# Half a conditioning batch moves from TensorE to VectorE, and VectorE may take two parts of such work at one unit of weights

## The reference, cut to what matters

```
cond = silu(c)
for l in range(2):
    mod = cond @ w_ada[l] + b_ada[l]
    sh1, sc1, g1, sh2, sc2, g2 = split(mod, 6)
    h = rms_norm(x) * (1 + sc1) + sh1
    z = h @ w_in[l]                        # all heads' inputs
    out_a = diff_attention(...)            # 6 heads, two softmaxes each
    out_b = latent_attention(...)          # 6 heads, one softmax each
    out_c = spatial_gating(...)
    x = x + g1 * (concat(out_a, out_b, out_c) @ w_out[l])
    h = rms_norm(x) * (1 + sc2) + sh2
    x = x + g2 * conv_ffn(h, w_up, conv, w_down)
```

## Time and profile before

| | before |
|---|---|
| median of 3 runs | 2416.82 us |
| profiled execution, its own time | 2413.93 us |
| its span (first to last instruction) | 2412.1 us |
| TensorE busy | 2318.8 us (96%) |
| VectorE busy | 1876.2 us (78%) |
| ScalarE busy | 1142.0 us (47%) |
| GpSimd busy | 293.0 us (12%) |
| granted clock of TensorE, mean | 0.987 of full speed |

### The profile page before, as it was taken

One profiled execution on the slowest core, in us unless ns is written; L12 is line 12 of the kernel. 1 busy time (PEld: TensorE's weight loads), 2 busy tenths in 40 slices (PEclk: granted clock), 3 DMA queues, 4 the chain that ended last, 5 costly groups with the idle time before them and its releaser, 6 DMA issues.

```text
span 2412.1 us, 37004 instructions
## 1 busy us (share of the span) xinstructions
PE 2318.8 (96%) x14736; PEld 2017.7 (84%) x14736; DVE 1876.2 (78%) x2585; ACT 1142.0 (47%) x1605; POOL 293.0 (12%) x437
## 2 busy tenths in 40 slices
PE   5889999999999999999999999999999999999999
PEld 2568888988888888888887899998888888888888
DVE  1557877879999999999997696667998667766775
ACT  1333665454543454435544366545554345544553
POOL 4231321221101100110021020001110000000000
PEclk9899999999999999999999999999999999999999
DMA  9998787968989988999896766445896566656664
GB/s 334 318 299 280 252 283 251 316 202 279 290 289 346 317 279 280 314 361 285 276 305 195 249 213 188 137 147 161 280 295 213 191 190 189 189 192 191 188 190 148
DMA packets 442459, 596.94 MB, mean 247 GB/s; under 512 B 24188, under 2 KB 381744, under 8 KB 442032
## 3 DMA queue, kind: packets, MB, share of 16 engines
q1 hardware_dynamic: 386592, 392.54, 50.4%
q0 software_dynamic: 55296, 201.35, 25.9%
q10 hardware_dynamic: 400, 0.71, 0.1%
HBM read 592.42 MB, written 2.10 MB: 246 GB/s over the span
## 4 chain that ended last, share of the span: by engine, by line
PE 76%; DVE 12%; issue 4%; DMA 4%; ACT 3%; POOL 0%; DVEq 0%; ACTq 0%; POOLq 0%
PE bank L1158 76%; DVE wlo L1735 4%; DMA ada<-in_w_ada_dram 3%; DVE acc L1729 3%; ACT whi L1488 2%; DVE T L1754 1%; DMA raw<-in_w_in_dram 1%; DVE T L1818 1%; ACT hx L1556 0%; DVE yg L1761 0%; DVE r L1803 0%; DVE hx L1839 0%; DVE yv L1761 0%; ACT sc_s L1609 0%; DVE mx L1771 0%
## 5 line engine op out<-in xcount | busy, mean ns | idle before, releaser
L1158 PE MATMUL bank<-hx,whi 128*128 128x512 f32 (+1 forms) x4480 | 1360.6, 363 | 4.5 <-DVE hx L1964 3.0
L1735 DVE TENSOR_TENSOR wlo<-raw,whi 128x1024 fp32r<-128x1024 f32 (+2 forms) x774 | 908.3, 1180 | 397.0 <-ACT whi L1488 395.1
L1488 ACT ACTIVATE whi<-raw 128x1024 fp32r<-128x1024 f32 (+2 forms) x774 | 778.7, 1017 | 749.5 <-PE bank L1158 623.0
L1158 PE MATMUL bank<-hx,wlo 128*128 128x256 f32 x3840 | 1089.0, 284 | 28.7 <-DVE hx L1839 20.6
L1158 PEld LDWEIGHTS bank<-hx,whi 128*128 128x128 f32 x4480 | 803.3, 189 | 142.7 <-issue 5.8
L1158 PEld LDWEIGHTS bank<-hx,wlo 128*128 128x128 f32 x3840 | 731.4, 190 | 48.0 <-issue 21.3
L1158 PE MATMUL bank<-mx,whi 128*128 128x512 f32 (+1 forms) x2096 | 613.0, 356 | 1.2 <-DVE xT L1785 1.2
L1158 PE MATMUL bank<-mx,wlo 128*128 128x256 f32 x1728 | 486.6, 282 | 2.6 <-DVE wlo L1735 2.6
L1158 PEld LDWEIGHTS bank<-mx,whi 128*128 128x128 f32 x2096 | 370.8, 189 | 60.9 <-issue 4.4
L1119 POOL DMA_DIRECT2D ada<-in_w_ada_dram x367 | 216.4, 591 | 1405.0 <-DVE acc L1729 1016.0
L1158 PEld LDWEIGHTS bank<-mx,wlo 128*128 128x128 f32 x1728 | 327.8, 190 | 5.1 <-DVE wlo L1735 4.1
(11 more groups left out here) (171 smaller groups left out, 1293.4 us busy)
## 6 DMA issues: line engine op xcount, KB each, us to landing
ada<-in_w_ada_dram POOLq DMA_DIRECT2D x367, 512.0 KB, 5.8
raw<-in_ffn_w_up_dram SPq DMA_DIRECT2D x352, 512.0 KB, 4.7
raw<-in_ffn_w_down_dram SPq DMA_DIRECT2D x176, 512.0 KB, 4.4
raw<-in_w_in_dram SPq DMA_DIRECT2D x128, 512.0 KB, 4.9
raw<-in_w_out_dram SPq DMA_DIRECT2D x48, 512.0 KB, 4.4
first_ada<-in_w_ada_dram POOLq DMA_DIRECT2D x17, 512.0 KB, 17.8
raw<-in_w_out_dram SPq DMA_DIRECT2D x32, 256.0 KB, 3.9
raw<-in_mla_w_uq_dram SPq DMA_DIRECT2D x12, 384.0 KB, 4.1
```

The costliest lines, as they stand in the source:

```text
L1158: return pe.matmul(out_, lhsT, rhs, start=start, stop=stop, skip_group_check=True)
L1488: return act.activation(out_, in_, ACT.Copy)
L1735: i_ = tt(dst, src, high.bitcast(F32), ALU.subtract)
```

## The change

Half 8, the first half of the fifth batch (batch 4), joins `VECTOR_HALVES`. Batch 4 is no longer mixed: its two halves now run one after the other, all of it on VectorE. And `ada` may place a second part at one unit if the debt is still at least 0.5 after the first was placed by a debt of a quarter or more; before the first `ffn` call that limit is set so high that it never applies again.

```diff
-VECTOR_HALVES = (5, 7, 9, 10, 11, 12, 13, 14, 15, 16, 17, 18, 19, 20, 21, 22, 23)
+VECTOR_HALVES = (5, 7, 8, 9, 10, 11, 12, 13, 14, 15, 16, 17, 18, 19, 20, 21, 22, 23)
...
-        self.pace, self.pace_debt = 1.0, 0.0
+        self.pace, self.pace_debt, self.two_from = 1.0, 0.0, 0.5
...
         if self.vector_next():
-            if self.ada_debt >= 0.25 and not (self.sums and self.half_begins()):
-                self.ada_debt -= 0.25
-                self.vector_part()
+            for due in (0.25, self.two_from):
+                if self.ada_debt >= due and self.vector_next() and not (self.sums and self.half_begins()):
+                    self.ada_debt -= 0.25
+                    self.vector_part()
...
     def ffn(self, l):
+        self.two_from = 1000
         blk, pb = 0, 0
```

## The result

The changed kernel takes 2432.84 us (median of four runs, 2431.97 to 2434.91), beside 2415.55 us of the kernel before in four runs: slower, by a ratio of 1.0076 (95% interval 1.0064 to 1.0089). The forecast of 2423.4 had the direction and less than half of the size; the time lies 1.8 us above the range. Its profiled execution has a span of 2431.3 us, 19.2 more than before.

What follows compares the result with a forecast made beforehand. VectorE was taken to bound latent attention, full DMA engines to delay the early burst, TensorE to bound behind. Late 3.4 less 1.9, early wait 3.4, next burst 0, clock 1.7: 6.6 us lost, 2423.4 us; range 2413 to 2431.

Steps and rivals of the forecast that it cites:

- the wait at the moved burst: Differential attention, burst now behind head 3's values: TensorE waits 3.4 us for its last load, between 2.3 and 8.1.
- the next burst: The burst following the moved one: its wait of 1.6 us stays unchanged, bounds -1.6 and +1.7 us.
- the end of the stretch: Behind the last head's low part: TensorE bounds again, so the fourth removed burst is a true gain of 1.87 us.
- Rival A: TensorE keeps the bound; VectorE takes the ten extra parts inside its reserve: 2409.8 us, faster, chance 0.14.
- The sign that was set for it: TensorE's waits between 413 and 490 us staying under 3 us would show that TensorE keeps the bound.
- the late term: First layer's latent attention, 413.2 to 480.2 us: VectorE's added parts make the stretch end 3.4 us later.
- All 9.2 us of waits are eaten: Same latent attention stretch: VectorE's 70.4 us of work fill all its waits, where the stretch took 67.0 us.
- Rival C: Half of VectorE's waits stay (4.6 us) and a second long TensorE wait drops the clock (1.7): 2429.7 us, chance 0.14.
- the wait that the prediction set at no cost: First part of half 9 waiting on TensorE's sum: hidden, since TensorE is ahead by the removed bursts; no cost.
- the early term: Differential attention, around 301 us: 3.4 us of waiting for the moved burst's load, plus 1.7 us of lower clock.
- The loads stay 512 KB each and equal in number: Conditioning loads: unchanged in size and count, so set at no cost.
- the clock: Behind the moved burst's 3.4 us wait: half speed for 3.4 us, taken once as 1.7 us, bounds zero to 3.4.

Runs made afterwards that it cites:

- the sum moved: Changed kernel with the sum of half 8 on TensorE placed ahead of unit 93's multiplication, not behind it and the following scores: 2430.64 us, ratio 1.0063.
- without pairs: Changed kernel with at most one part at a unit everywhere, half 8 still on VectorE: 2429.66 us, ratio 1.0061.
- thin parts: Changed kernel with ten parts of half 8 and all sixteen of half 9 computed on 64 of 1024 columns: 2419.35 us, ratio 1.0018.
- The run with half bytes: Changed kernel with half of the bytes left out of eleven conditioning loads, issued from 267 to 300 us: 2431.34 us, ratio 1.0065.
- The run with ten thin parts: Changed kernel with ten of half 8's sixteen parts computed on 64 of 1024 columns: 2428.56 us, ratio 1.0051.

## Why the prediction was wrong

*Right.* The direction; the parts' 31.4 us on VectorE (31.5) and its work of 70.4 (69.6); the wait at the moved burst (3.4 forecast; 3.7 in three pieces, and 0.3 ahead of them) and the lower clock behind it; the next burst no worse (its wait of 1.6 us went, the lower bound); the end of the stretch, 1.9 forecast and 1.7 measured between units 101 and 115. Rival A is ruled out: TensorE waits 12.9 us from 424 to 501 us by the list. The sign that was set for it, under 3 us between 413 and 490 us, could hardly come: the kernel before already waits 3.2 us there, the 1.5 of the earlier trace rows and the 1.7 for rotated queries that they leave out.

*Wrong, the late term (3.4 us; 10.0 measured).* It failed at the step "All 9.2 us of waits are eaten", and the 3.4 was taken "because the waits are all for engines that would now be ahead". 7.4 us of waits stayed. Rival C, which kept 4.6, had the mechanism. 3.5 of them are the wait that the prediction set at no cost: "TensorE is ahead there by the bursts it no longer has". TensorE was not ahead; it had been waiting for VectorE. And a part right behind another starts 0.1 us late, where the lower bound had allowed for overlap. VectorE's waits between units 83 and 101 were 11.2 us before, 6.7 in the changed kernel, 4.5 with the sum moved, 7.7 without pairs: with 57 to 72 us of work they never fell under 4.5. That part of the 9.2 was no reserve, and the runs without pairs and with thin parts show that the rest decides: the stretch lasts as long as VectorE's work and 4.5 to 8.7 us, or the 63.6 that TensorE needs without bursts, whichever is longer. The run with ten thin parts lies above this (62.4 us of work, 73.9 in all): it is faster than the changed kernel up to unit 93, and as slow behind it.

*Wrong, the early term (3.4 for the wait, 1.7 for the clock; 8 to 9 measured).* The prediction put the wait down to one load's latency behind the part that frees its buffer, and set "The loads stay 512 KB each and equal in number" at no cost. They are equal in number in the whole, not ahead of unit 57. That the DMA engines are full stood in the earlier trace rows and was given no price. By the landing times in the traces, 21 conditioning loads land between the starts of units 45 and 57 in the changed kernel, 15 in the kernel before: six more of 512 KB, 3.1 MB, at the 360 to 388 GB/s of the two full rows 8.1 to 8.7 us. The run with half bytes took 2.9 MB out and 7.6 to 7.8 us with them. The wait of 3.7 us met the forecast by chance: the load took 7.1 us, not 5.1, but the burst began 1.65 us later than thought. The Trainium skill ("DMA: Bandwidth & Descriptors", section Bandwidth) gives about 358 GB/s as a core's rate when both cores of an HBM domain stream. The program here runs on one core: the row at 360 lies at that figure, the row behind it, at 388, above it.

*Wrong, the clock (one loss of 1.7 us).* The rows of the changed kernel give 3.5 us by unit 57 and three more losses of 1.7 to 1.8 up to unit 101: 8.8 in all. Where the extra matmuls kept 7.1 of them away, the median fell by 2.3 us, hardly clear of the spread, and the one profile by 5 to 7: the term was too small by the rows, and how much of it is time stays open.

*Not forecast.* 2 to 3 us between units 57 and 83, where VectorE runs 15 parts for 12 before: five of half 8's stand at units 78 to 82. The cause stays open.

## What to carry to other kernels

An engine's waits in a stretch where three engines hand work to and fro are not its reserve: add work, and some stay, so price the stretch as its work and those waits. Work moved forward brings its bytes forward: count the loads that must land before the next fixed point, and divide by the rate of the full stretch, before asking for one load's latency. Where an accumulator is emptied by one engine and filled by another, look for what stands ahead of the emptying in that engine's own queue.

## What the runs showed of the hardware

A lower granted clock did not show at its face value: extra matmuls kept it up where the rows had 7.1 us lost, and the median fell by 2.3 us; in the kernel before, of three comparisons two show no gain and one 0.13%. VectorE was busy 24.55 of 28.5 us there; what the clock costs where TensorE alone sets the pace, no run here shows. A part that follows another on the same accumulator starts 0.10 us after it ends (466.68 + 0.76 = 467.44, and the next starts at 467.54), and the 24 such parts of the late stretch have 0.9 us of waits ahead of them; other instructions start 0.09 us before the end of a part.
